# Moving weights stored even columns first, read by TensorE from two halves in turn

## What is computed

```python
qa, ka, va, qi, ki, wi, qb, kb, vb = _split(xn @ w_in, EVEN_SPLITS)
...
return y @ w_out
...
return (jax.nn.silu(g) * u) @ w_down
...
x = x + (jax.nn.silu(gt) * up) @ w_down[i]
...
x = x + jax.nn.sigmoid(rms_norm_2(x, g_pl[i]) @ w_pl_gate[i]) * pl
```

## Time and profile before

| | |
|---|---|
| median of 3 runs | 1243.9 us (1239.71 to 1246.34) |
| the profiled execution's own time | 1232.83 us |
| its span from first to last instruction | 1230.7 us |
| TensorE busy (matmul) | 1206.7 us, 98% of the span, 8616 matmuls |
| VectorE / ScalarE / GpSimd busy | 841.3 / 702.8 / 320.6 us |
| granted TensorE clock, mean | 0.994 of full speed |
| weights loaded | 189 MB by SyncE's queue |

### The profile page before, as it was taken

The page is one execution under the profiler, slowest core; times in us unless marked ns, Lnnn a source line. Parts: engine busy times, 40 slices in busy tenths (PEclk is TensorE's granted clock), DMA queues, the critical chain, the costliest instruction groups (busy, mean ns, idle before and its releaser), DMA issues.

```text
span 1230.7 us, 21370 instructions
## 1 busy us (share of the span) xinstructions
PE 1206.7 (98%) x8616; PEld 1105.0 (90%) x8616; DVE 841.3 (68%) x1507; ACT 702.8 (57%) x1181; POOL 320.6 (26%) x257
## 2 busy tenths in 40 slices
PE   9999999999999999999999999999999999999997
PEld 7776899998877799998899999999989989999886
DVE  6795588884675578885468787788854565555457
ACT  5465476653457566664366667667667445444344
POOL 2172200000015400000056676675555320000000
PEclk9999999999999999999989999999999999999999
DMA  7633355555453355555343322322222646555542
GB/s 285 240 140 135 120 206 205 185 183 198 169 178 134 115 210 210 201 195 201 123 142 133 138 104 104 138 104 104 79 93 104 222 156 230 200 182 201 188 155 85
DMA packets 31586, 199.74 MB, mean 162 GB/s; under 512 B 4289, under 2 KB 6481, under 8 KB 8706
## 3 DMA queue, kind: packets, MB, share of 16 engines
q1 hardware_dynamic: 29506, 189.27, 42.6%
q0 software_dynamic: 1840, 8.60, 1.8%
q10 hardware_dynamic: 144, 0.52, 0.1%
HBM read 197.33 MB, written 1.05 MB: 161 GB/s over the span
## 4 chain that ended last, share of the span: by engine, by line
PE 87%; DVE 7%; ACT 3%; issue 2%; POOL 1%; DMA 0%; POOLq 0%; ACTq 0%; DVEq 0%
PE ps L1144 25%; PE ps L1145 24%; PE ps L1146 24%; PE ps L1519 1%; PE ps L1535 1%; DVE ps L2776 1%; PE ps L1297 1%; PE ps L1316 1%; PE ps L1151 1%; PE ps L1284 1%; PE ps L1168 1%; DVE conv L2713 1%; PE ps L1237 1%; DVE wlo L2328 1%; PE ps L1541 1%
## 5 line engine op out<-in xcount | busy, mean ns | idle before, releaser
L1144 PE MATMUL ps<-halves,whi 128*128 128x256 f32 x1472 | 413.8, 281 | 0.1
L1145 PE MATMUL ps<-halves,whi 128*128 128x256 f32 x1472 | 408.5, 278 | 0.0
L1146 PE MATMUL ps<-halves,wlo 128*128 128x256 f32 x1472 | 408.4, 277 | 0.0
L2328 DVE TENSOR_TENSOR wlo<-raw,whi 128x2048 fp32r<-128x2048 f32 (+1 forms) x133 | 301.4, 2268 | 119.7 <-ACT whi L1798 116.1
L1798 ACT ACTIVATE whi<-raw 128x2048 fp32r<-128x2048 f32 (+1 forms) x143 | 269.9, 1889 | 110.1 <-PE ps L1146 107.3
L1144 PEld LDWEIGHTS ps<-halves,whi 128*128 128x128 f32 x1472 | 277.3, 188 | 0.6 <-DVE halves L2915 0.3
L1145 PEld LDWEIGHTS ps<-halves,whi 128*128 128x128 f32 x1472 | 277.3, 188 | 0.1
L1146 PEld LDWEIGHTS ps<-halves,wlo 128*128 128x128 f32 x1472 | 277.0, 188 | 0.0
L1085 POOL TENSOR_TENSOR wlo<-raw,whi 128x1024 fp32r<-128x1024 f32 x72 | 173.9, 2423 | 53.2 <-ACT whi L1807 52.7
L979 POOL TENSOR_TENSOR rstd<-sumsq,half_power 128x1 f32<-128x1 f32 x14 | 11.1, 793 | 589.0 <-ACT xn L1825 417.2
L1144 PE MATMUL ps<-whi,halves 128*128 128x512 f32 (+4 forms) x440 | 151.9, 345 | 3.9 <-DVE halves L2430 3.7
(11 more groups left out here) (337 smaller groups left out, 1852.4 us busy)
## 6 DMA issues: line engine op xcount, KB each, us to landing
raw<-in_stream SPq DMA_DIRECT2D x176, 1024.0 KB, 4.8
gain<-in_gains POOLq DMA_DIRECT2D x7, 512.0 KB, 5.7
bias<-in_rel POOLq DMA_DIRECT2D x1, 1536.0 KB, 8.6
raw<-in_stream SPq DMA_DIRECT2D x2, 648.0 KB, 7.2
cst<-in_consts POOLq DMA_DIRECT2D x1, 1280.5 KB, 6.1
raw<-in_stream SPq DMA_DIRECT2D x2, 528.0 KB, 4.2
x<-in_x SPq DMA_DIRECT2D x2, 512.0 KB, 4.3
out<-xn SPq DMA_DIRECT2D x4, 256.0 KB, 2.2
```

The lines of the kernel that those rows point to most:

```text
L1144: nc.tensor.matmul(out, a_hi, b_hi, start=start, stop=False)
L1145: nc.tensor.matmul(out, a_hi, b_lo, start=False, stop=False)
L1146: return nc.tensor.matmul(out, a_lo, b_hi, start=False, stop=stop)
L2328: dve.tensor_tensor(used(wlo, n), used(raw, n), used(whi, n).bitcast(F32), ALU.subtract)\
```

## The change

In the slots of kinds "columns" and "down", each group of columns that a matmul may read (512, 324 or 264) is packed with its even columns first and its odd ones behind them. The load, the split into `whi` and `wlo`, the buffers and the waits are as before. TensorE reads the moving operand through a view, `in_order`: column 0 of the first half, column 0 of the second, column 1 of the first, and so on, so that the output's columns stand in PSUM in their usual order. Consecutive entries that the moving operand reads thus lie 1024 bytes apart for 512 columns (648 for 324, 528 for 264), and every second entry is the neighbour of the last but one. For the gate's two units of 256 columns the view takes 128 entries out of each half. No instruction is added or removed.

```diff
+def evens_first(a):
+
+    return np.concatenate([a[..., 0::2], a[..., 1::2]], -1)
...
                 at += c
+            view[:, :, 0:at] = evens_first(view[:, :, 0:at])
...
-            view = out[n].reshape(P, 2, D)
-            view[:] = w[args[0] * 256:args[0] * 256 + 256].reshape(2, P, D).transpose(1, 0, 2)
+            rows = w[args[0] * 256:args[0] * 256 + 256].reshape(2, P, 2, 512).transpose(1, 0, 2, 3)
+            out[n].reshape(P, 2, 2, 512)[:] = evens_first(rows)
...
+            def in_order(ap, a=0, n=None):
+
+                both = ap.rearrange("p (b c) -> p c b", b=2)
+                return both if n is None else both[:, a // 2:(a + n) // 2, :]
...
-                    w = slice(cols.start - b * 512, cols.stop - b * 512)
+                    w = (cols.start - b * 512, cols.stop - cols.start)
...
-                                     wh[:, k, w], wl[:, k, w], kt == 0, kt == KT - 1)
+                                     in_order(wh[:, k, :], *w), in_order(wl[:, k, :], *w), kt == 0, kt == KT - 1)
...
-                                 wh[:, k, :], wl[:, k, :], kt == 0, kt == KT - 1)
+                                 in_order(wh[:, k, :]), in_order(wl[:, k, :]), kt == 0, kt == KT - 1)
...
-                                 wh[:, k, c], wl[:, k, c], g == 0 and k == 0, g == 3 and k == 1)
+                                 in_order(wh[:, k, c]), in_order(wl[:, k, c]), g == 0 and k == 0, g == 3 and k == 1)
...
-                                         a_lo[:, kt, t * P:(t + 1) * P], wh[:, k, c], wl[:, k, c],
+                                         a_lo[:, kt, t * P:(t + 1) * P], in_order(wh[:, k, c]), in_order(wl[:, k, c]),
...
-                                     wh[:, kt, c], wl[:, kt, c], kt == 0, kt == 1)
+                                     in_order(wh[:, kt, c]), in_order(wl[:, kt, c]), kt == 0, kt == 1)
```

## The result

The changed kernel is a little faster: 1227.31 us (median of 4 runs, 1223.21 to 1229.27) against 1243.28 us (4 runs, 1239.71 to 1246.34). The ratio is 0.9882, 95% interval 0.9847 to 0.9917, thus 16 us or 1.2% less, a small change but one clear of the noise. The forecast was 1591 us; the profiled execution took 1223.21 us, its span is 1221.3 us.

What follows compares the result with a forecast made beforehand. TensorE's intake of columns was taken as the bound; 336.7 us for 512-column matmuls plus 15.5 for narrower ones, less 5 for gaps, gave +347 on 1243.9, thus 1591 us; own range 1565 to 1645, 8-in-10 range 1238 to 1645.

Steps and rivals of the forecast that it cites:

- What bounds the kernel: Down stages and attention layers: TensorE's intake of columns sets the end, so any change in matmul cost goes straight there.
- The counts, and that nothing else is touched: 1800 of 8616 matmuls change, 1656 of 512 columns; loads, instructions, waits and PSUM outputs stay the same.
- The price of a hop, bounded: Changed matmuls: reading entries 1024 bytes apart in turn takes 430 ns per 512 columns, 203.3 more than 226.7.
- the half pace: Case chosen for the changed matmuls: an entry takes two cycles, 430 ns per 512 columns, 1591 us in all; chance 0.58.
- the float32 pace: Float32 matmuls at L1480: 215 ns a record, 0.84 ns per column, taken as TensorE's half pace for 4-byte entries.
- the 6% lost by ordered reads: Down0: 512 columns take 226.7 ns against 213.3 at 2.4 GHz; read as a reader close to its limit.
- hops are free: Rival for the changed matmuls: reading two places in turn costs nothing, step stays 226.7 ns, 1244 us; chance 0.21.
- the 13.3 ns go away: Rival: moving reads no longer meet stationary-tile reads, saving 13.3 ns per 512-column matmul, 1220 us; chance 0.09.
- The sum: All changed matmuls: 336.7 us for 512 columns plus 15.5 for narrower ones, less 5 for swallowed gaps, +347 us.

Runs made afterwards that it cites:

- probe3: Changed kernel plus a tail of matmuls with other steps, start entries, bf16 and moving tokens, 20 of most forms; one execution of 1379.24 us.
- probe2: Changed kernel plus a tail of matmuls read in turn with steps 2 and 4, from four to 64 places, and float32; one execution of 1353.51 us.
- probe1: Changed kernel plus a tail of 24 matmuls per form, varying read order, distance, width and stationary tile; span 1372.6 us.
- before_again: The kernel before, unchanged, run once more for a second trace; 1237.49 us, ratio 1.0004.
- after_again: The changed kernel, unchanged, run once more for a second trace; 1222.87 us against 1237.53, ratio 0.9887.

## Why the prediction was wrong

**What bounds the kernel: right.** The changed matmuls lie on the path that sets the end. 10.9 ns less for each of 264 showed as 2.8 to 2.9 us in each down stage, with none lost to a wait. In the attention layers and the gate it was right only in part: there some of the gain, or all of it, went into waits (below).

**The counts, and that nothing else is touched: right in the instructions, wrong in one effect.** 1656 + 144 matmuls, and no other engine or transfer came to matter. But "Up0 and the delta rule's rounds keep their steps of 113 to 118 ns and their lengths" failed for up0, which took 118 ns where it had taken 113.3.

**"The price of a hop, bounded": the step that failed.** I took 430 ns, and my reason was that "a reader that close to its limit hardly has room for fetching each 4-byte entry from another place than the last. It probably fetches two or four neighbours at once, and the change takes the neighbour away". The first half fits the runs: lines of 16 bytes give the rows of float32r with one or two places read entry by entry, and where the neighbour is really taken away, the half pace comes out, 452.5 ns with every 2nd entry of one stream. The step that failed is the second half, that this change takes the neighbour away: a matmul of 512 columns got 10.9 ns cheaper (215.8) and not 203.3 dearer. The neighbour that counts is not the entry read last but the last but one. The rows that fit only so are 227.5 ns at a distance of 2 against 215.8 at 4 and more, 226.5 with two places and step 2, and 340 with step 3. Reading in turn doubles what each lane gets from a line. That there are two lanes is a theory that gives these rows and forecast six of seven in probe3; the rows that it misses stand in probe2 and probe3.

The Trainium skill, "SBUF — State Buffer", in the part on the DMA ports, has the lines of 16 bytes and a penalty for each new one, and the runs agree. It also has two hits on a line as enough for full bandwidth, and there they differ: every 2nd entry of one stream hits each line twice in a row and took 452.5 ns, and the change, which goes to another line at every entry, took 215.8. The runs decide.

The row on which I leaned, the float32 pace, was of another kind: float32 with two passes gets slower in turn (539.5 against 429 ns), float32r does not. The row that spoke for the truth was in my own list, the 6% lost by ordered reads. I read it as a reader at its limit, which a harder pattern must push over. It was rather a pattern that fits the reader badly, which another one can mend.

**The rival "hops are free": the right mechanism, with the wrong price.** Its words, that TensorE "keeps the two places apart" and "finds a1 in what it fetched for a0", are what the two lanes amount to. It took the time as unchanged, because it left the 6% where they were.

**The rival "the 13.3 ns go away": it was what happened, for another reason.** Its 1220 us lie 7 us from the median measured, at a chance of 0.09. The size was near (10.9 ns of 13.3 at 512 columns, 7.5 to 9 of those at the narrower ones). Its reason, moving reads that meet those of the stationary tile, fell with probe1: a tile of 32 columns loses as much as one of 128.

**The sum.** What 16 us are made of: 984 of the 512-column matmuls lie outside the attention layers, 984 x 10.9 = 10.7 us. The 672 in the attention layers stepped at 230 ns before (42.95 to 45.25 us, ten steps) and step at 215.8 now, up to 672 x 14 = 9.4 us, and the 144 narrower ones give 1.2. That makes 21 us as the upper bound. Of it an attention layer gave 3.4 us rather than 5, since part of it went into waits (the second layer of the first pair, the first of the second, 140.6 to 137.2 us), and the gate's part nothing, since in the tail waits set the end. Against some 16.5 us stand 4.7 us for each up stage at the slower pace. The first profiled pair is 9.4 us apart, and that closes: 16.5, less 4.7 for up0 and less 2.4 because its first attention layer gave only 1.0. The second pair (before_again, after_again) is 5.9 us apart, with two slower stages. The medians are 16.0 and 14.7 apart. Single executions scatter by 6 to 18 us, so what the medians show above the traces is not placed.

**What stays open.** Why a stretch of ordered matmuls runs at 113 or 118 ns, and why it is the slower one more often once the stages around it are read in turn. What is seen: it follows the pace of `early` ahead of it; other engines, DMAs, a stationary tile that stays or moves, and single matmuls between are not needed for the slower pace, and a dip of the granted clock just ahead is not enough for it (before_again had 0.91 from 100 to 120 us and stayed at 113). The place of the moving tokens was never varied. A phase between the reader's lines and the matmuls' turn would fit, but that is only argued. Open is also why three or more places in turn (274.5, 291.5, 489.5 and 431.5 ns for 4, 6, 8 and 64), runs of two to 32, bf16 and float32 in turn come out as they do.

## What to carry to other kernels

Compare the step between starts with columns through the clock: the 6% more on a busy TensorE were here a cost of how the operand is read, and the layout removed it without an instruction. For float32r, read the moving operand from two places in turn, both in order and at least 4 entries apart, but never with a step over 1 in one stream, nor in runs of two; for bf16 and float32 leave it in order. And read an untouched stage again after a change: here one gave back nearly 5 us at a time, and the remedy was to treat its matmuls alike.

## What the runs showed of the hardware

- A new line of 16 bytes costs TensorE's moving reads 1.77 ns: 452 / 256, 226.5 / 128 and 340 / 192 ns for float32r, 451 / 256 and 900 / 512 for bf16, the lines counted by the theory of lanes. It is a time and not a count of TensorE's cycles: of the matmuls that read bf16 with step 8 the first three took 2.70 us (1274.41 to 1277.11) at a granted clock of 1.00, the last three also 2.70 us (1289.71 to 1292.41) at 0.50, the lower level, 1.2 GHz. Windows of probe3 there:

```profile
1274.40:1278.00 3.60, 3.60 (x5) 0.47 (x4) 0.00 (x0) 0.00 (x0) 0.00 (x0) 1.00 0.00 0
...
1288.00:1292.40 4.40, 4.40 (x6) 0.54 (x5) 0.00 (x0) 0.00 (x0) 0.00 (x0) 0.50 0.00 0
```

- The clock fell there although TensorE shows as busy for the whole of each stretch: it took in one column in 1.76 ns (900 / 512).
- Matmuls read in turn step at their columns at 2.4 GHz and 2.2 to 2.5 ns more, from 512 down to 264 columns (215.8, 202.5, 189.2, 162.5, 137.2, 135.8 and 112.5 ns for 512, 480, 448, 384, 324, 320 and 264). Those of 256 columns take 111.8, 5.1 ns more than 106.7, so something other than columns sets that step.
- Ordered reading of 256 float32r columns has three paces, 113.3, 118 and 120 ns, each held over a whole stretch without a break (some 930 matmuls in the up stages); read in turn there is one, 111.5 to 111.8 ns.
